# A decoder block with product-key experts: the order of the first table's units, and where the last of their results are kept

## What is computed

```python
def peer_ffn(x, w_q, sub_keys, u_tab, v_tab):
    ...  # 8 heads pick 16 experts each for every token, with a softmax weight (gate)
    u = jnp.take(u_tab, ec, axis=0)
    act = jax.nn.gelu(jnp.einsum('cd,chkd->chk', xc, u), approximate=False)
    wgt = gc * act
    v = jnp.take(v_tab, ec, axis=0)
    return jnp.einsum('chk,chkd->cd', wgt, v)
```

## Time and profile before

| | us |
|---|---|
| median of three runs | 3862.97 (3860.53 to 3867.95) |
| the profiled execution | 3854.19 |
| its span, first to last instruction | 3852.4 |
| TensorE busy | 3753.8 (97%) |
| VectorE busy | 2716.0 (71%) |
| ScalarE busy | 1384.7 (36%) |
| transfers | 1234.84 MB, mean 321 GB/s |

### The profile page before, as it was taken

The page is one execution under the profiler, slowest core; times in us unless marked ns, Lnnn a source line. Parts: engine busy times, 40 slices in busy tenths (PEclk is TensorE's granted clock), DMA queues, the critical chain, the costliest instruction groups (busy, mean ns, idle before and its releaser), DMA issues.

```text
span 3852.4 us, 60802 instructions
## 1 busy us (share of the span) xinstructions
PE 3753.8 (97%) x24487; PEld 3474.4 (90%) x24487; DVE 2716.0 (71%) x3363; ACT 1384.7 (36%) x1969; POOL 1140.0 (30%) x595
## 2 busy tenths in 40 slices
PE   8999999999999999999999999999999899999997
PEld 8999999999988888888888899999999877878886
DVE  4544555456688755656555588888888788888988
ACT  5544444444423100000000344566663334444443
POOL 0000000000734443534443473233233334233431
PEclk9999999999999999999999999999999999999999
DMA  5344554554589999999999559999999999999996
GB/s 189 110 153 178 184 185 181 181 184 175 220 360 385 403 422 403 402 397 404 392 409 376 208 183 395 381 393 386 379 381 422 402 399 402 391 375 393 402 393 245
DMA packets 193198, 1234.84 MB, mean 321 GB/s; under 512 B 20160, under 2 KB 37136, under 8 KB 49936
## 3 DMA queue, kind: packets, MB, share of 16 engines
q1 hardware_dynamic: 107792, 657.56, 44.4%
q0 software_dynamic: 73728, 536.90, 34.2%
q10 hardware_dynamic: 11520, 38.28, 2.5%
HBM read 1194.39 MB, written 37.75 MB: 320 GB/s over the span
## 4 chain that ended last, share of the span: by engine, by line
PE 84%; DMA 8%; DVE 6%; issue 1%; ACT 1%; SPq 0%; ACTq 0%; DVEq 0%
PE dense_ps L941 22%; PE dense_ps L930 13%; PE dense_ps L932 13%; PE dense_ps L931 13%; PE dense_ps L1181 7%; DMA wbuf<-in_w_units_dram 4%; PE score_ps L1181 3%; PE dense_ps L973 3%; DMA wbuf<-in_peer_v_dram 3%; PE oT_ps L1181 2%; PE o_ps L1181 2%; DMA row<-in_peer_v_dram,expert 2%; PE o_ps L1066 1%; DVE h L1238 1%; PE score_ps L1138 1%
## 5 line engine op out<-in xcount | busy, mean ns | idle before, releaser
L1284 DVE TENSOR_TENSOR w_lo<-wbuf,w_hi_r 128x1024 fp32r<-128x1024 f32 x800 | 972.7, 1222 | 552.9 <-ACT w_hi_r L581 551.6
L581 ACT ACTIVATE w_hi_r<-wbuf 128x1024 fp32r<-128x1024 f32 x872 | 917.5, 1059 | 1158.4 <-PE dense_ps L932 555.8
L930 PE MATMUL dense_ps<-act_hi,w_hi_r 128*128 128x256 f32 x4128 | 1181.4, 286 | 26.4 <-DVE w_lo L1284 25.8
L931 PE MATMUL dense_ps<-act_lo,w_hi_r 128*128 128x256 f32 x4128 | 1171.4, 284 | 0.0
L932 PE MATMUL dense_ps<-act_hi,w_lo 128*128 128x256 f32 x4128 | 1171.3, 284 | 0.0
L930 PEld LDWEIGHTS dense_ps<-act_hi,w_hi_r 128*128 128x128 f32 x4128 | 795.7, 193 | 35.9 <-DVE w_lo L1284 26.4
L931 PEld LDWEIGHTS dense_ps<-act_lo,w_hi_r 128*128 128x128 f32 x4128 | 795.8, 193 | 0.0
L932 PEld LDWEIGHTS dense_ps<-act_hi,w_lo 128*128 128x128 f32 x4128 | 795.3, 193 | 0.0
L941 PE MATMUL dense_ps<-xT,wbuf 128*128 128x256 f32 x3136 | 686.4, 380 | 0.8 <-ACT xT L566 0.8
L941 PEld LDWEIGHTS dense_ps<-xT,wbuf 128*128 128x128 f32 x3136 | 593.1, 190 | 85.6 <-issue 5.3
L532 POOL DMA_INDIRECT row<-in_peer_v_dram,expert x199 | 417.7, 2099 | 805.4 <-DVE h L1238 780.5
(11 more groups left out here) (241 smaller groups left out, 4328.5 us busy)
## 6 DMA issues: line engine op xcount, KB each, us to landing
wbuf<-in_w_units_dram SPq DMA_DIRECT2D x456, 1024.0 KB, 6.6
wbuf<-in_peer_v_dram SPq DMA_DIRECT2D x128, 1024.0 KB, 9.2
act_spill<-stage ACTq DMA_DIRECT2D x64, 256.0 KB, 8.9
gate_spill<-gbuf ACTq DMA_DIRECT2D x8, 2048.0 KB, 10.5
e_act<-act_spill SPq DMA_DIRECT2D x32, 512.0 KB, 9.7
e_gate<-gate_spill SPq DMA_DIRECT2D x32, 512.0 KB, 11.6
row<-in_peer_u_dram,expert POOLq DMA_INDIRECT x256, 13.7
row<-in_peer_v_dram,expert POOLq DMA_INDIRECT x199, 11.1
```

Of the source, the lines that this page charges most:

```text
L581: act.activation(w_hi[:, j, :], wbuf[n % 2][:, j, :], ACT.Copy).then_inc(w_hi_ready, 1)
L930: nc.tensor.matmul(out, w[0], x[0], start=opens, stop=False)
L931: nc.tensor.matmul(out, w[0], x[1], start=False, stop=False)
L1284: V.tensor_tensor(w_lo[n % 2][:, j, :], wbuf[n % 2][:, j, :], w_hi[:, j, :].bitcast(F32), ALU.subtract).then_inc(lo_by_dve, 1)
```

## The change

The units of the first table are rotated by four (`np.roll` of the laid out table by `-KEPT`), so that unit j holds the experts of V group (j+4)//2, and the last four units hold those of groups 0 and 1. ScalarE writes the Gelu of these four units straight into `e_act[0]` and `e_act[1]`, without `stage` and without a spill. SP no longer loads groups 0 and 1, and its wait for the last spills stands before the load of group 2. The spills of the other units go to a place two groups further on. Since a group that is kept is complete only with its second unit, each product of group and gates, and with it each high part and low part of a group, stands one unit later in the orders of VectorE and ScalarE, for the kept groups and for all others. The order of SP's list is otherwise as before.

```diff
--- before.py
+++ after.py
@@ -57,6 +57,7 @@
 U_UNITS = 64
 N_V = N_U + U_UNITS
 GROUPS = 32
+KEPT = 4
 GCHUNK = 32
 STATS_AT, SD_AT, APPLY_AT, OUT_AT = (19, 62), (21, 62), (24, 63), (27, 63)
 RES_AT = (10, 24)
@@ -460,24 +461,18 @@
                     load(N_U + c, 2, i)
             for j in range(U_UNITS - 8, U_UNITS):
                 load(N_U + j)
-                if j == U_UNITS - 8:
-                    for k in range(4):
-                        sp.wait_ge(act_sent[k], 16)
-                    load_act(0)
                 if j == U_UNITS - 7:
                     sp.wait_ge(gate_sent, 16 * (HALF // GCHUNK))
                     load_gates(0, 0)
                 if j == U_UNITS - 6:
                     load_gates(0, 1)
-                if j == U_UNITS - 5:
-                    load_act(1)
                 if j == U_UNITS - 4:
                     load_gates(1, 0)
             load(N_V)
+            for j in range(4):
+                sp.wait_ge(act_sent[j], 16 * ((U_UNITS - KEPT) // 4))
             load_e(2)
             load(N_V + 1)
-            for j in range(4):
-                sp.wait_ge(act_sent[j], 16 * (U_UNITS // 4))
             for g in range(4):
                 load(N_V + 2 + 2 * g)
                 load_e(3 + g)
@@ -606,17 +601,21 @@
 
                 n = N_U + j
                 act.wait_ge(dense_ready, n + 1)
-                if j >= 4:
-                    act.wait_ge(act_sent[n % 4], 16 * (j // 4))
-                act.activation(stage[n % 4][:, :, :], dense_ps[n % 4][:, :, :], ACT.Gelu).then_inc(dense_out, 1)
-                act.wait_ge(dense_out, n + 1)
-                act.dma_start(act_spill[j // 2, :, (j % 2) * 2 * HALF:(j % 2 + 1) * 2 * HALF],
-                              stage[n % 4][:, :, :].rearrange("p c t -> p (c t)")).then_inc(act_sent[n % 4], 16)
+                half = slice((j % 2) * 2, (j % 2 + 1) * 2)
+                if j >= U_UNITS - KEPT:
+                    act.activation(e_act[j // 2 % 2][:, half, :], dense_ps[n % 4][:, :, :], ACT.Gelu).then_inc(dense_out, 1)
+                else:
+                    if j >= 4:
+                        act.wait_ge(act_sent[n % 4], 16 * (j // 4))
+                    act.activation(stage[n % 4][:, :, :], dense_ps[n % 4][:, :, :], ACT.Gelu).then_inc(dense_out, 1)
+                    act.wait_ge(dense_out, n + 1)
+                    act.dma_start(act_spill[(j + KEPT) // 2, :, half.start * HALF:half.stop * HALF],
+                                  stage[n % 4][:, :, :].rearrange("p c t -> p (c t)")).then_inc(act_sent[n % 4], 16)
                 for g in placed:
                     place_move(g)
                 split_hi(n + 1, 3)
-                if n + 3 - N_V >= 0 and (n + 3 - N_V) % 2 == 0:
-                    move_e((n + 3 - N_V) // 2)
+                if n + 2 - N_V >= 0 and (n + 2 - N_V) % 2 == 0:
+                    move_e((n + 2 - N_V) // 2)
                 for k in range(3):
                     split_hi(n + 2, k)
                 g = G_PER * (j + 1 - G_FIRST)
@@ -861,13 +860,13 @@
 
             act.activation(ident_r[:, :], ident[:, :], ACT.Copy).then_inc(ident_ok, 1)
             for j in range(4):
-                act.wait_ge(act_sent[j], 16 * (U_UNITS // 4))
+                act.wait_ge(act_sent[j], 16 * ((U_UNITS - KEPT) // 4))
             for m in range(U_UNITS):
                 n = N_V + m
                 if m + 1 < U_UNITS:
                     split_hi(n + 1, 3)
-                if m % 2 and m + 3 < U_UNITS:
-                    move_e((m + 3) // 2)
+                if m % 2 == 0 and m + 2 < U_UNITS:
+                    move_e((m + 2) // 2)
                 for j in range(3) if m + 2 < U_UNITS else ():
                     split_hi(n + 2, j)
                 for t in range(TILES):
@@ -1653,7 +1652,10 @@
 
             def e_mult(q):
 
-                dve.wait_ge(e_in[q % 2], 16 * (q // 2 + 1))
+                if q < KEPT // 2:
+                    dve.wait_ge(dense_out, N_V - KEPT + 2 * q + 2)
+                else:
+                    dve.wait_ge(e_in[q % 2], 16 * (q // 2))
                 dve.wait_ge(gates_in[q // 2 % 2], 32 * (q // 4 + 1))
                 e = e_act[q % 2][:, :, :].rearrange("p b (c t) -> p b c t", c=HALF // GCHUNK)
                 gates = e_gate[q // 2 % 2][:, :, 4 * (q % 2):4 * (q % 2) + 4, :].rearrange("p c b t -> p b c t")
@@ -1687,20 +1689,20 @@
                     if 0 <= g < HALF // 4:
                         for k in range(G_PER):
                             one_hots(g + k)
-                    if n + 4 >= N_V and n % 2 == 0:
-                        e_mult((n + 4 - N_V) // 2)
-                    if n + 4 >= N_V and n % 2:
-                        e_rest((n + 3 - N_V) // 2)
+                    if n + 3 >= N_V and n % 2:
+                        e_mult((n + 3 - N_V) // 2)
+                    if n + 2 >= N_V and n % 2 == 0:
+                        e_rest((n + 2 - N_V) // 2)
 
                 section(n, between)
 
             for m in range(U_UNITS):
 
                 def between():
-                    if m % 2 == 0 and m + 4 < U_UNITS:
-                        e_mult(m // 2 + 2)
                     if m % 2 and m + 3 < U_UNITS:
-                        e_rest((m + 3) // 2)
+                        e_mult((m + 3) // 2)
+                    if m % 2 == 0 and m + 2 < U_UNITS:
+                        e_rest((m + 2) // 2)
 
                 section(N_V + m, between)
                 for t in range(TILES):
@@ -1759,7 +1761,7 @@
     parts.append(_np.stack([cb, cc, ch], 1).reshape(-1, 2, P, KT * P))
     parts.append(twos(gc, _units(wc)))
     parts += [_units_by_k(wo), _units(wq)]
-    parts.append(_units(_np.asarray(inputs["peer_u"])[0].T))
+    parts.append(_np.roll(_units(_np.asarray(inputs["peer_u"])[0].T), -KEPT, 0))
     return _np.ascontiguousarray(_np.concatenate(parts).reshape(-1, P, KT * P))
```

## The result

The changed kernel is **slower**: 3904.02 us (median of 4 runs, 3899.4 to 3907.03) against 3863.61 for the kernel before, a ratio of 1.0105 with a 95% interval of 1.0092 to 1.0117. The forecast was 3860.0, its range ended at 3870.0. The profiled execution took 3906.9 us, its span is 3905.1.

The account below looks back on a forecast made before the run. The prediction took transfers to bound the stretch around the seam. Its terms, -3.7 - 1 + 1.5 + 0.5 + 0 + 1, gave about -2 us, rounded to -3: 3851.2 profiled, 3860.0 as median, range 3850 to 3870.

Parts of the forecast that it names:

- What bounds the kernel: End of first table and seam: bound by transfers, not arithmetic; from 3500 to 3600 us TensorE busy throughout at full clock.
- a cover of 1.5 us: Steady part: the odd unit's low part is ready at 3557.8, TensorE starts that unit at 3559.3, 1.5 us later.
- The bytes removed: Around the seam: two group loads and four spills fewer, 2.10 MB, worth 3.7 us gained, between 0 and 5.0.
- the third rival: At the seam: the bytes removed were not those waited for, total within 1.5 us of before, 3862; chance 0.12.
- The clock: Behind the pauses near 3063 and 3121: shorter pauses still drop the clock; 1 us gained, ends 0 and 6.6.
- VectorE's order: Second table: products and low parts one unit later, low part ready just in time; 0 us, ends 0 and 2.
- The seam's list: SP's queue at the seam: first weight halves issued later, costing 1.5 us for unit 1 and 0.5 for unit 3.
- All later groups: Steady part, 29 groups: weight half issued 3.0 us later, landing moves little; 1 us lost over all, ends 0 and 15.
- The second rival: Steady part: SP held by the low part becomes a standing stall, +13 to +24 us, 3876 to 3887; chance 0.17.
- SP's queue hardly runs dry: Steady part: the half issued before is still in flight when the group's load goes, so the landing moves little.
- The first rival: At the seam: pauses shrink under the point where the clock falls, -9 to -12 us, 3851 to 3854; chance 0.25.

Follow-up runs that it names:

- the eleventh experiment: Changed kernel with later groups' products, high and low parts in their old places, groups 2 and 3 loaded between the halves of V units 1 and 3: ratio 0.9982.
- the tenth: Changed kernel with each load of a group and its gates placed between the two halves of the next odd unit's weights: ratio 0.9998.
- The eighth experiment: Kernel before, with SP held ahead of each group's load until VectorE has made the product standing where the changed kernel has the low part: ratio 1.0142.
- third experiment: Kernel before with only the move of products, high parts and low parts by one unit, groups 0 and 1 still spilled and loaded: ratio 1.0148.
- The first experiment: Changed kernel with products, high and low parts of groups 2 to 31 back in their old places, groups 0 and 1 kept on chip: ratio 1.0000.
- fifth: Changed kernel with later groups' products, high and low parts in their old places, groups 2 and 3 loaded behind V units 1 and 3: ratio 0.9994.

## Why the prediction was wrong

Step by step:

- **What bounds the kernel**: right for the seam. Wrong in what it left unsaid of the steady part: the earlier trace rows has TensorE at 100 of 100 us and the transfers at 1.00 and 393 GB/s side by side. I took from it that there is "little to win and a cover of 1.5 us to lose" and did not ask how little it takes to make the transfers the bound.
- **The bytes removed, 3.7 us**: of the right order. The first table takes 821.9 to 826.0 us in the six kernels with kept groups, mean 823.8, and 825.8 to 829.9 in the seven without, mean 827.9: 4.1 us, single executions though, and between the changed kernel and the one before there is none (826.0 and 825.9). Of the 3.7 us only 2.5 were foretold for this stage; the other 1.2 were to come off the pause behind it. In whole runs a gain shows in the eleventh experiment alone, and not in the tenth, where the loss is gone too. So the third rival, that these bytes were not waited for, is not excluded for whole runs.
- **The clock, 1 us**: too little. The pauses were foretold at 5.4 and 6.2 us and are 6.73 and 4.88. Windows of 10 us from the end of each pause, before and after, have the granted clock ahead of the last two numbers:

```profile
3063.00:3073.00 10.00, 9.61 (x58) 9.62 (x59) 10.00 (x7) 4.57 (x6) 3.70 (x3) 0.67 0.92 346
3121.00:3131.00 10.00, 9.60 (x30) 7.65 (x31) 10.00 (x7) 4.27 (x6) 3.36 (x2) 0.67 1.03 408
```

```profile
3069.00:3079.00 10.00, 9.62 (x67) 9.62 (x68) 10.00 (x7) 4.51 (x6) 3.71 (x3) 0.81 0.95 366
3123.00:3133.00 10.00, 8.92 (x30) 6.61 (x31) 10.00 (x7) 5.65 (x7) 3.35 (x2) 0.83 0.99 401
```

  0.67 and 0.67 became 0.81 and 0.83: some 5.6 us less of slow work, at 54% a gain of 3 us. The fall itself stayed, as said. Left out altogether was the clock in the steady part, an estimated 7 us of the loss (above).
- **VectorE's order, 0 us**: right within what can be measured. The eighth experiment, low parts early, costs as much as the third, low parts late; from 3110 to 3800 us TensorE waits for a group's low part twice in the changed kernel, 5.6 us in all.
- **The seam's list, 2 us**: of the right order. The first experiment, which holds SP only there, has no gain; mending the seam (fifth and eleventh) brings 0.06 to 0.18%, 2 to 7 us, with intervals of 4 us either way.
- **All later groups, 1 us with an end of 15**: this is the step that failed. The sum took "the group goes at 3544.5 and the weight half at 3545.9, 3.0 us later" from the old trace by putting the new low part where the product had been, as if that place stayed fixed. It doesn't: the instruction ahead of it in VectorE's order is the low part of the even unit's first quarter, which waits for that unit's weights, which stand in the queue that is now held. SP stood 11.3 us instead of the 7 that follow from these times, and the weight half went 7.5 us later, not 3.0, in a loop that keeps itself going. The sum then let "the landing" of that half move "little". From the issue of the half before it to its landing it is 18.1 us before (3537.47 to 3555.52) and 20.9 after (3567.04 to 3587.95): 2.9 us more, against a cover of 1.5. "SP's queue hardly runs dry" was false too: it was empty from 3576.99 to 3578.76.
- **The second rival** named the right mechanism, its place, and the point from which it decides (SP's queue empty when the group's load is issued). Its price, 13 to 24 us, was too low, since each half was again charged a fixed delay of at most 3.0 us; 40 were measured, and 55 for the move alone. Its chance, 0.17, looks too small now: it was a wait set ahead of the scarce transfers, with a cover of 1.5 us.
- **The first rival**, that the pauses shrink until the clock no longer falls, did not come: the clock fell behind 6.73 and 4.88 us.

The Trainium skill, "DMA: Bandwidth & Descriptors", section "Anatomy of one DMA — SWDGE (gpsimd) path", says that a semaphore wait happens on the issuing sequencer before dispatch and not in the transfer engines. That section is on transfers that GpSimd issues; the trace agrees for SP's: the group's load waited for a low part 147.5 us in 13 times, and the weights behind it waited with it, though their own buffers were free (both halves go within 1.00 us from 3580.01).

## What to carry to other kernels

When an instruction is moved later, follow who waits for it until the path ends or comes back. Here low part, SP, weights, low part was a circle, and what it takes beyond the time of the work is paid in every round; a fixed delay read off the old trace (3.0 us) leaves out what the circle adds (7.5). In a hand-written transfer list, a load that waits for a computed result must not stand ahead of loads that the same computation needs; putting it between two loads where the second has to wait anyway took the loss from 1.05% to nothing that can be measured (0.9998).

An engine that is 100% busy beside transfers that are 100% busy has little cover to give away: here a hold of 153 us in 28 rounds, 5.5 us each, was free, and one of 264 us, 9 us each, was not. Look at both before putting a wait at nothing.

## What the runs showed that was not expected

- A hold is free up to a point and then paid for in large part: 153 us of SP's waits cost nothing that can be measured, 264 us cost 0.72%, 310 us 1.42%.
- Keeping two groups on chip, 2.1 MB, was worth 0.43% while the list was held (third experiment against the changed kernel, 1.0148 and 1.0105, each against its own runs of the kernel before) and 0.0 to 0.2% where it wasn't. Why so much in the held list was not tried.
- Moving only the group loads behind a weight load, with no wait added, cost 0.23%: the place in the queue matters also without a hold.
- A shorter pause does not always spare the clock. In the first table of the changed kernel a pause of only 2.43 us, ended at 3024.96, was followed by some 3.4 us of work at the lower level (granted clock 0.54, 0.50, 0.50 and 0.75 in the four windows of 1 us from 3025), as much as the pause of 4.53 us in the earlier trace rows.
